# Swapped rows by transfers, probabilities in halves and a last norm by token in a four-layer trunk

## The reference

```python
def _rmsnorm(x, g):
    y = x * lax.rsqrt(jnp.mean(x * x, axis=-1, keepdims=True) + RMS_EPS)
    return y * g
def _rope(x, positions, rot_dim):      # local attention: rot_dim 16 of 64
    x1, x2 = xr[..., :half], xr[..., half:]
    rot = jnp.concatenate([x1 * cos - x2 * sin, x2 * cos + x1 * sin], axis=-1)
def _swa(h, positions, w_in, b_in, sinks, w_o, b_o):   # 16 query heads, 4 key heads, window 2 chunks of 64
    q, k, v = jnp.split(h @ w_in + b_in, ...)
    q, k = _rope(q), _rope(k)
    s = q @ k * 64 ** -0.5 ...          # masked before the first chunk
    p = softmax(concat([s, sink]))[..., :-1]
    return (p @ v) @ w_o + b_o
def reference(...):
    for i in range(4):
        x = x + mixer(_rmsnorm(x, norm_mix[i]))
        x = x + jnp.square(jax.nn.relu(_rmsnorm(x, norm_mlp[i]) @ w1)) @ w2
    return _rmsnorm(x, norm_final)
```

## Time and profile before

| | us |
|---|---|
| median of three runs (2105.13 to 2106.68) | 2105.22 |
| the profiled execution | 2105.36 |
| its span | 2103.6 |
| outside the span, 2105.36 - 2103.6 | 1.76 |

### The profile page before, as it was taken

How to read it: one execution, slowest core, us unless ns; L and a number is a source line. 1 busy time by engine, 2 the same in 40 slices (tenths; PEclk the granted TensorE clock), 3 DMA queues, 4 the chain that set the end, 5 groups by cost and what they waited for, 6 DMA issues and landing times.

```text
span 2103.6 us, 25082 instructions
## 1 busy us (share of the span) xinstructions
PE 2068.6 (98%) x9798; PEld 1697.5 (81%) x9798; DVE 1162.0 (55%) x1384; ACT 814.9 (39%) x1160; POOL 187.1 (9%) x224
## 2 busy tenths in 40 slices
PE   8999999999999999999999999999999999999997
PEld 6778888888878888888877788888887888888886
DVE  6765543443887743444767654444476756344344
ACT  6564322323466423222455432232345644232231
POOL 6102000000200200004200100000321011000000
PEclk9999999999999999999999999999999999999998
DMA  6222323223322332223221233223232122322321
GB/s 184 61 66 75 101 95 100 97 93 100 110 70 91 105 96 100 95 94 101 83 81 51 75 106 100 95 95 101 95 99 57 61 80 91 100 97 92 100 90 41
DMA packets 120560, 190.62 MB, mean 91 GB/s; under 512 B 15520, under 2 KB 34848, under 8 KB 120480
## 3 DMA queue, kind: packets, MB, share of 16 engines
q1 hardware_dynamic: 116784, 185.78, 27.5%
q0 software_dynamic: 1280, 2.62, 0.5%
q10 hardware_dynamic: 2416, 1.12, 0.2%
HBM read 184.78 MB, written 2.10 MB: 89 GB/s over the span
## 4 chain that ended last, share of the span: by engine, by line
PE 90%; DVE 5%; ACT 3%; issue 1%; DMA 1%; SPq 0%; POOL 0%; DVEq 0%; ACTq 0%
PE psum L535 28%; PE psum L537 28%; PE psum L536 28%; PE psum L839 1%; DVE w_lo L1218 1%; ACT arena L2161 1%; PE psum L948 1%; PE psum L812 1%; DVE small L1513 0%; ACT arena L2149 0%; DMA x<-in_x 0%; PE psum L1065 0%; PE psum L1095 0%; PE psum L800 0%; PE psum L637 0%
## 5 line engine op out<-in xcount | busy, mean ns | idle before, releaser
L1218 DVE TENSOR_TENSOR w_lo<-w_raw,w_hi 128x1024 fp32r<-128x1024 f32 x343 | 423.5, 1240 | 787.1 <-ACT w_hi L1954 786.6
L1954 ACT ACTIVATE w_hi<-w_raw 128x1024 fp32r<-128x1024 f32 x343 | 362.3, 1061 | 957.1 <-PE psum L537 956.9
L535 PE MATMUL psum<-h_hi,w_hi 128*128 128x512 f32 x1384 | 547.0, 395 | 0.7 <-DVE w_lo L1218 0.7
L537 PE MATMUL psum<-h_hi,w_lo 128*128 128x512 f32 x1384 | 538.9, 389 | 0.0
L536 PE MATMUL psum<-h_lo,w_hi 128*128 128x512 f32 x1384 | 538.8, 389 | 0.0
L535 PE MATMUL psum<-u_hi,w_hi 128*128 128x512 f32 x1320 | 516.6, 391 | 1.7 <-DVE u_lo L1393 1.4
L537 PE MATMUL psum<-u_hi,w_lo 128*128 128x512 f32 x1320 | 514.0, 389 | 0.0
L536 PE MATMUL psum<-u_lo,w_hi 128*128 128x512 f32 x1320 | 513.9, 389 | 0.0
L535 PEld LDWEIGHTS psum<-h_hi,w_hi 128*128 128x128 f32 x1384 | 259.9, 188 | 58.5 <-issue 4.3
L536 PEld LDWEIGHTS psum<-h_lo,w_hi 128*128 128x128 f32 x1384 | 259.9, 188 | 56.7 <-issue 4.1
L537 PEld LDWEIGHTS psum<-h_hi,w_lo 128*128 128x128 f32 x1384 | 259.8, 188 | 54.4
(11 more groups left out here) (249 smaller groups left out, 1418.5 us busy)
## 6 DMA issues: line engine op xcount, KB each, us to landing
w_raw<-in_mlp_w SPq DMA_DIRECT2D x256, 512.0 KB, 3.7
w_raw<-in_mla_w_o SPq DMA_DIRECT2D x16, 512.0 KB, 3.5
w_raw<-in_lru_w_in SPq DMA_DIRECT2D x16, 512.0 KB, 3.9
w_raw<-in_swa_w_in SPq DMA_DIRECT2D x12, 512.0 KB, 3.7
w_raw<-in_mla_w_ukv SPq DMA_DIRECT2D x8, 512.0 KB, 4.5
w_raw<-in_lru_w_out SPq DMA_DIRECT2D x8, 512.0 KB, 3.5
w_raw<-in_swa_w_o SPq DMA_DIRECT2D x8, 512.0 KB, 3.5
w_raw<-in_mla_w_in SPq DMA_DIRECT2D x7, 512.0 KB, 3.7
```

Of the source, the lines that this page charges most:

```text
L535: nc.tensor.matmul(out, stat[0], mov[0], start=start, stop=False, skip_group_check=skip)
L537: return nc.tensor.matmul(out, stat[1], mov[0], start=False, stop=stop, skip_group_check=skip)
L1218: nc.vector.tensor_tensor(w_lo[:, to], w_raw[:, to], exact(w_hi[:, to]), ALU.subtract).then_inc(w_ready, 1)
L1954: nc.scalar.activation(w_hi[:, to], w_raw[:, to], ACT.Copy).then_inc(w_hi_done, 1)
```

## The change

Two places of the program change.

In the local attention the ten row swaps leave TensorE. GpSimd clears two tiles (`swa_k_sw`, and `rot` of 128x1024) and then issues four transfers of eight rows for the keys and four for each query, from the biased rows into the cleared tile. VectorE takes cos times the rows and sin times the transferred tile. The keys' rotation now stands behind a `split(1)` on VectorE. The queries use areas 3, 2 and then 0, and give the bank back at `rows_in`; scores 0 to 4 go into area 1, 5 to 7 into area 2. The probabilities are normalised in two halves, the first after four of the eight exponentials, and transposed in two halves of four; ScalarE copies both turned halves, VectorE none. Two of the four banks of the output's first product stand ahead of scores 5.

At the end the last unit of the last MLP finishes bank by bank, and `add_last` scales and adds one chunk of 512 at a time instead of two. ScalarE makes the gained chunks (`gained_rows`). The last two squares are added on VectorE; the token sums go to bank 1 of area 1, three quarters of them ahead of `last_squares`. Then TensorE transposes all 32 blocks, so that tokens are on partitions; ScalarE scales token blocks 0 and 2, VectorE 1 and 3, in halves of 512 features, and SyncE stores each half (128x512, 256 KB), eight stores. The row-wise `spread` is gone, and the output is tokens by features, so the host turns nothing.

```diff
+        QUERY_AREA = [3, 2] + 6 * [0]
+        SCORES_AREA = 5 * [1] + 3 * [2]
...
-            for p in range(KC // 2):
-                sp.wait_ge(out_ready, p + 1)
-                sp.dma_start(A["out"][p * 256:(p + 1) * 256, :].rearrange("(a p) n -> p a n", p=P),
-                             two(arena[:, p * PAIR:(p + 1) * PAIR])).then_inc(stored, 16)
-            sp.wait_ge(stored, 16 * (KC // 2))
+            def store(b, at):
+                sp.dma_start(A["out"][b * P:(b + 1) * P, at], out_rows[b][:, at]).then_inc(stored, 16)
+
+            for pair in range(2):
+                for n, at in enumerate(HALVES):
+                    sp.wait_ge(out_act, 2 * pair + n + 1)
+                    store(2 * pair, at)
+                    sp.wait_ge(out_dve, 2 * pair + n + 1)
+                    store(2 * pair + 1, at)
+            sp.wait_ge(stored, 16 * 8)
...
+                    if last and kp == 3:
+                        order = [(kk, m) for m in range(4) for kk in range(2)]
...
+                        if last and kp == 3 and n in (1, 5):
+                            mm.then_inc(last_bank, 1)
...
-                    claim(2)
-                    pe.wait_ge(area_free[3], c.at("area3"))
-                    jobs["swa", "scores area", i] = c.now("area2")
+                    to = SCORES_AREA[i]
+                    claim(to)
...
-                    c.add("p")
-                    pe.wait_ge(p_ready, c.now("p"))
                     p = swa_m["p"][:, (i % 2) * W_ATT:(i % 2 + 1) * W_ATT]
-                    claim(2)
-                    claim(3)
-                    jobs["swa", "turned areas", i] = c.now("area2"), c.now("area3")
-                    for k in range(2 * QB):
-                        mm = nc.tensor.transpose(area(2)[:, k * P:(k + 1) * P], p[:, k * P:(k + 1) * P], ident)
-                    mm.then_inc(psum_done, 1)
-                    summed("transposes", i)
+                    for half in range(2):
+                        c.add("p")
+                        pe.wait_ge(p_ready, c.now("p"))
+                        if half == 0:
+                            claim(2)
+                        for k in range(half * QB, (half + 1) * QB):
+                            mm = nc.tensor.transpose(area(2)[:, k * P:(k + 1) * P], p[:, k * P:(k + 1) * P], ident)
+                        mm.then_inc(psum_done, 1)
+                        summed("transposes", i, half)
...
-                swap_keys()
                 query(1)
-                swap_query(0)
                 query(2)
-                swap_query(1)
 
                 for i in range(5):
                     scores(i)
...
                         weighted(i - 1)
                     query(i + 3)
                     transposes(i)
-                    swap_query(i + 2)
-                swap_query(KC - 1)
+                out(0, (2, 3))
...
+                    def turn(b, half):
+                        for k in range(4 * half, 4 * half + 4):
+                            mm = nc.tensor.transpose(area(b)[:, k * P:(k + 1) * P], gx[k][:, b * P:(b + 1) * P], ident)
+                        mm.then_inc(turned, 1)
...
+                    claim(1)
+                    pe.wait_ge(squares_added, c.now("squares_added") + 3)
+                    sums(0, ssq)
+                    pe.wait_ge(squares, before + 6)
+                    sums(1, late_squares[0])
+                    sums(2, late_squares[1])
+                    pe.wait_ge(last_squares, 1)
+                    sums(3, late_squares[2]).then_inc(psum_done, 1)
...
+                    pe.wait_ge(gained_x, KC)
+                    turn(0, 0)
+                    turn(0, 1)
+                    turn(1, 0)
+                    claim(1)
+                    turn(1, 1)
...
+                def rotate(i):
+
+                    q, swapped = chunk(m["q"], i), chunk(m["rot"], i % 2)
+                    dve.wait_ge(swa_q_swapped[i % 2], 64 * (i // 2 + 1))
+                    nc.vector.tensor_tensor(swapped, swapped, sin[:, :], ALU.mult)
                     link(nc.vector.tensor_tensor(q, q, cos[:, :], ALU.mult))
-                    nc.vector.tensor_tensor(q, q, chunk(scratch, i % 2), ALU.add).then_inc(mixed, 1)
+                    nc.vector.tensor_tensor(q, q, swapped, ALU.add).then_inc(mixed, 1)
+
+                def rotate_keys():
+
+                    dve.wait_ge(swa_k_swapped, 64)
+                    nc.vector.tensor_tensor(two(swa_k_sw), two(swa_k_sw), twice(sin[:, :]), ALU.mult)
+                    link(nc.vector.tensor_tensor(two(kraw), two(kraw), twice(cos[:, :]), ALU.mult))
+                    nc.vector.tensor_tensor(kraw, kraw, swa_k_sw, ALU.add).then_inc(k_rotated, 1)
...
+                def normalised(i, half):
+                    if half == 0:
+                        dve.wait_ge(half_exp_done, i + 1)
+                    else:
+                        dve.wait_ge(area_free[SCORES_AREA[i]], jobs["swa", "scores area", i])
...
-                    if i <= 5:
-                        rotate_swapped(i + 1)
-                    if i == 5:
-                        rotate_swapped(7)
                     largest(i)
-                    if i <= 5:
-                        rotate_rest(i + 1)
-                    if i == 5:
-                        rotate_rest(7)
+                    if i < KC - 1:
+                        rotate(i + 1)
                     if i >= 1:
                         head_lo(UHI[i - 1], ULO[i - 1])
-                    normalised(i)
+                    normalised(i, 0)
+                    normalised(i, 1)
                     if i + 3 < KC:
                         rows_in(i + 3)
                     split(1)
-                    done("transposes", i)
-                    nc.vector.tensor_copy(m["pt"][:, 0:T], bank(2, 0)).then_inc(area_free[2], 1)
...
+            def add_last():
+
+                for k in range(4, 8):
+                    if k == 4:
+                        dve.wait_ge(last_bank, 1)
+                    elif k == 5:
+                        sum_ready()
+                    elif k == 6:
+                        dve.wait_ge(last_bank, 2)
+                    else:
+                        units_passed(4)
+                    t = chunk(mlp_m["scaled"], k - 4)
+                    ins = nc.vector.tensor_tensor(t, bank(k // 2, k % 2), rstd2[:, :], ALU.mult)
+                    if k % 2:
+                        free(ins, k // 2)
+                        dve.wait_ge(area_free[k // 2], c.at(f"area{k // 2}"))
+                    else:
+                        link(ins)
+                    nc.vector.tensor_tensor(chunk(x, k), chunk(x, k), t, ALU.add
+                                            ).then_inc(x_ready if k % 2 else x_late, 1)
...
-                for k in range(KC):
-                    ins = nc.vector.tensor_scalar(chunk(arena, k), chunk(x, k), col("norm_final", k), None, ALU.mult)
-                link(ins)
-                norm_columns(rstd4, 2, D)
...
+                nc.vector.tensor_tensor(late_squares[2], late_squares[2], late_squares[3], ALU.add
+                                        ).then_inc(last_squares, 1)
...
-                for p in range(KC // 2):
-                    t = two(chunk(arena, 2 * p, 2))
-                    nc.vector.tensor_tensor(t, t, twice(bank(2)), ALU.mult).then_inc(out_ready, 1)
...
+                for b in (1, 3):
+                    for half, at in enumerate(HALVES):
+                        dve.wait_ge(turned, 2 * b + half + 1)
+                        nc.vector.tensor_scalar(out_rows[b][:, at], area(b)[:, at], rstd4[:, b:b + 1], None, ALU.mult
+                                                ).then_inc(out_dve, 1)
...
+            def gained_rows(k):
+                nc.scalar.activation(gx[k], chunk(x, k), ACT.Copy, scale=col("norm_final", k)).then_inc(gained_x, 1)
...
+                    for half in range(2):
+                        done("transposes", i, half)
+                        ins = nc.scalar.activation(m["pt"][:, half * T:(half + 1) * T], bank(2, half), ACT.Copy)
+                    ins.then_inc(area_free[2], 1)
...
+                if kind == "swa":
+                    g.memset(swa_k_sw, 0.0)
+                    g.memset(swa_m["rot"], 0.0).then_inc(swa_cleared, 1)
+                    pool.wait_ge(swa_cleared, 1)
+
+                    def swap_rows(to, rows, swapped):
+                        for at in (0, SW_D):
+                            for a, b in ((at, at + 8), (at + 8, at)):
+                                g.dma_start(to[a:a + 8, :], rows[b:b + 8, :]).then_inc(swapped, 16)
+
+                    pool.wait_ge(biased, 2)
+                    swap_rows(swa_k_sw, swa_m["p"][:, 0:W_ATT], swa_k_swapped)
+                    for k in range(KC):
+                        pool.wait_ge(biased, 2 + k + 1)
+                        if k >= 2:
+                            pool.wait_ge(mixed, 1 + k - 1)
```

(1 more changed line is left out.)

192 lines of the change are left out of this document (112 added, 80 removed).

## The result

The changed kernel takes 2087.72 us (median; 2086.95 to 2088.25), the kernel before 2105.18 in the same session: ratio 0.9917, 95% interval 0.9899 to 0.9935. One execution of the changed kernel (4690 us) and, in the session of the first four experiments, one of the kernel before (6642 us) took over twice as long as all others and are left out. Forecast was 2088.9, range 2086.5 to 2093.0. The profiled execution has a span of 2086.4 us against 2103.6, 17.2 less, and lies 1.85 outside it (1.76 before). From the spread of the sums ahead of the attention (L637 before, L663 after) to the first output product of pair 7 the trace shows 106.33 before and 94.48 after: 11.85 off. From E, the end of the last product, to the end of the span it shows 19.6 and 14.2: 5.4 off. Together 17.25, all of it.

What follows compares the result with a forecast made beforehand. TensorE, busy 98% of the span, was taken to bound the kernel. 2105.36 - 11.4 (attention) - 4.9 (end) = 2089.1 us for the profiled execution; the median, 0.14 lower, gives 2088.9, range 2086.5 to 2093.0.

Steps and rivals of the forecast that it cites:

- Attention, 11.4 off: Local attention: TensorE sheds 14.1 us of swap passes and waits, new waits cost 2.7, net 11.4 us off.
- the 8.6 of the sum: Local attention: 20 float32 swap passes leave TensorE at 0.43 us each, 8.6 us off.
- Swaps ready in 3.7 us: Attention swaps by transfer: rows ready 0.3 + 1.5 + 1.9 = 3.7 us after the bias, at worst 5.4.
- eight us to spare: Attention loop, once running: a query's swapped rows have eight us to spare between its bias and its rotation.
- S + 11.8: S is the start of a head pair's scores; the forecast put the next query's rotation at S + 10.4 + 1.4.
- from 10 the loop pays too: Rival, slower than before: GpSimd transfers over 12 us each; from 10 the loop loses too; 2110 at 13; chance 0.04.
- End, 4.9 off: Behind the last product: span ends at E + 14.7 instead of E + 19.6, 4.9 us off.
- the step on the clock: End transposes: half clock stays to the end, 32 x 0.23 = 7.4 us, last half turned at E + 11.4.
- clock kept or given back: Rival at the end: TensorE keeps or regains full clock during the transposes, 2087.7 us; chance 0.11.
- Small stores: Rival at the end: 256 KB stores at two thirds of the rate, 1.7 us less gained, 2090.6; chance 0.05.
- stay at 10.4: Rival in the attention loop: swaps go but VectorE and ScalarE hand over slower, loop keeps 10.4 us, 2094.3; chance 0.05.
- the swap of 8 us: Late swaps rival, worse case: 8 us per swap, keys 3.2 and query 1 2.6 later, 2095.5; late swaps' chance 0.11.

Runs made afterwards that it cites:

- the first four experiments: Changed kernel again (2087.41 us), its attention part only (2092.66), its end part only (2100.38), and with remaining waits at start and end attacked (2087.82).
- the second trace: Profile of the changed kernel run once more, nothing edited, beside the kernels with one part each: 2087.41 us, ratio 0.9915.
- the three traces with 6.8 us at 0.50: Changed kernel with start edits and four transposes earlier (2087.82 us), with sixteen two-row transfers per swap (2101.45), with two more VectorE copies per loop pair (2090.47).
- attention alone: Only the attention part of the change (rotary rows by transfers, probabilities in halves), the end as in the kernel before: 2092.66 us, ratio 0.9941.

## Why the prediction came out right

- **Time.** 2087.7 against 2088.9, in the range; 17.2 us less in the span against 16.3 forecast. The attention is right by its mechanism. The end is right in its first half, and in its second by two errors that partly cancel.
- **Attention, 11.4 off: right, 11.85.** The swaps' passes are gone; one of them put back costs 0.85 a pair, so the 8.6 of the sum was real work on the path. The loop is 8.68 (8.75), bound by TensorE, and VectorE's spare was 0.4 (0.5). The new waits: 0.87 at the first scores (0.75), 0.68 at query 3 (0.75), 0.11 and 0.36 at pair 5 (0.25 and 0.6), 0.29 at pair 7 (0.25). Pair 5 is nearly all that the sum had too much.
- **Swaps ready in 3.7 us: too low, and at the start it was luck that it cost nothing.** By the landing times of the nine sets in the first trace the rows were there 3.8 to 5.6 us behind the end of their bias, 4.5 in the median, as a transfer landed in 2.4 and not 1.9. No rotation waited, but query 1's set landed at 1089.16 and its rotation began at 1089.18 (1.0 of room in the second trace). Two us later costs 4.1 us, not 2.0: the price of lateness at the start was too low, as the landing took 3.4 and not 2, and the clock fell behind the wait. In the loop a set was there 5.3 to 6.3 us ahead of its rotation. The forecast's "eight us to spare" is not what its own figures give (wanted at S + 11.8, bias at S + 1.7, 3.7 for the set: 6.4); its rival's "from 10 the loop pays too" fits the one wait of 0.55 with sixteen transfers. That rival put the kernel's break-even at sets of about 12 us; the attention's own is reached at 9 to 11, from first issue to last landing.
- **End, 4.9 off: 5.4 in the first trace, 5.9 in the second; the step on the clock was wrong.** Sums at E + 4.1 (3.8) and scale at E + 5.8 (5.5) are 0.3 late, as the last eight sums took 1.19 and VectorE was released later than added up. But the half clock was taken to stay to the end, 32 transposes at 0.23, 7.4 us. It came back after 3.4 us; the transposes took 5.2 and 5.4, the last was scaled by E + 10.2 and not E + 12.1, and the last bytes are then set by the stores. That is the rival "clock kept or given back", which said 2087.7 and was given 0.11. What came behind the transposes was too short in the sum, and this hid the error: in the three traces with 6.8 us at 0.50 the span ended 4.2 to 4.5 us behind the last transpose, where the forecast had 3.3, as VectorE's last two scalings and SyncE's last three stores stand in a row there. Had the half clock stayed, the transposes at their 0.21 would end at E + 11 and the span at some E + 15.3 (both estimates from these traces), 4.3 off and not 4.9. The rule behind the forecast, from the Trainium skill, "TensorE: Matmul & The Clock Gate", Part 4, that transposes don't count as activity for the full clock, does not hold here for float32 transposes (the times that it gives beside it are for bf16): in the first trace the clock returned at 2079.3 in a run of float32 transposes that had begun at 2076.19. What misled me was that the trace of before shows no transposes at its end, only sums and idle time, and I read its half clock on.
- **Small stores: no loss.** Eight of 256 KB moved 382 GB/s, as the four of 512 KB of before; four of 512 KB with rows twice as long moved 405. The Trainium skill, "DMA: Bandwidth & Descriptors", Bandwidth, asks for 1 MiB or more a transfer for three quarters of peak, behind a table of loads that GpSimd issued. These stores were issued by SyncE with several in flight, and a loss between 512 and 256 KB is not seen, nor the two thirds of the rate which the rival took.
- **The other rivals.** The loop did not stay at 10.4; and swaps slow enough to make the kernel slower were not reached with sixteen transfers each. Two of their sums are added wrong: with the swap of 8 us, 2088.9 + 3.2 + 2.6 is 2094.7 and not 2095.5, and 8.2 + 7.9 + 5 is 21.1 and not 21.5. Neither bears on the forecast or its range.
- **Not taken apart.** Of the parts of the new end (bank by bank, squares added on VectorE, scaling by token, eight stores) only the stores were varied, so how its 5.4 us divide is argued from the traces alone.

## What to carry to other kernels

Where one engine bounds a loop, moving its smallest helper work to a transfer is worth its full duration only as long as the next chain has room: compute that room (0.4 us here), and test both engines by adding work to each. The transfers' lateness is the other limit: here the attention's gain was gone once a set took 9 to 11 us. A transfer that a steady loop hides is bare at the loop's start: price its lateness there, with the clock that falls in the wait. At the end of a kernel, count back from the last byte stored; what ends before the stores do is free, and what stands ahead of the first store is not.

## What the runs showed of the chip

- The granted clock came back to 1.00 in gapless float32 transposes of 128 columns, 3.4 or 6.8 us after it fell, in ten traces; the transposes came 0.21 us apart before it and 0.11 after. In the old end, with sums, idle time and two dense products (attention alone), it stayed at 0.50 for 16 us.
- The length of the end behind the last product varied by 1.4 us (E + 13.6 to E + 15.0) over ten traces with the same new end, but for one with its transposes reordered, and went with where the clock fell and how long it stayed down. Differences of this end below that are not to be read from one trace.
- A wait of 2.1 us of TensorE was enough for the scores behind it to run slow in part (1.74 in place of 1.10 us), 7.4 us for all of them (1.98).
- GpSimd issues a transfer of a few rows within SBUF in 0.50 us whether it has 8, 4 or 2 rows, and they landed in 2.4, 2.0 and 1.6 us in the median, so the number of transfers sets when the rows are there.
- Stores of 512 KB and of 256 KB with rows of 2 KB in HBM moved the same 382 GB/s; stores of 512 KB with rows of 4 KB moved 405 (one trace).
